# q and k kept as whole fp32 numbers in a hybrid attention and Fourier layer: one fp32 product on quarters of the array in place of three split products

## The reference

```python
h = rmsnorm(x, norm_g)
proj = h @ w_in                       # q, k, v, g_attn, u, g_four
q = rmsnorm(q.reshape(B, S, 12, 64), q_g)
k = rmsnorm(k.reshape(B, S, 12, 64), k_g)
for window, dil in ((128, 1), (512, 4), (2048, 16)):
    # keys gathered by stride dil, band of 64 on each side of the query
    s = einsum('brnqhd,brnkhd->brnhqk', qb, kb) / 8 + bias
    o, lse = softmax(s) @ v, logsumexp(s)
attn = merge of the three by softmax(lse), times silu(g_attn)
four = Re(fft2(u)) @ w_four, times silu(g_four)
y = x + concat[attn, four] @ w_out
```

## Time and profile before

| | us |
|---|---|
| median of three runs | 3880.73 |
| the profiled execution, time | 3869.16 |
| the profiled execution, span from first to last instruction | 3867.4 |
| setup, weights and first half, up to about 1133 | 1133 |
| second half, up to about 2189 | 1056 |
| attention, first score at 2214.3, last product at 3251.8 | 1037 |
| combine | 616 |

### The profile page before, as it was taken

The page is one execution under the profiler, slowest core; times in us unless marked ns, Lnnn a source line. Parts: engine busy times, 40 slices in busy tenths (PEclk is TensorE's granted clock), DMA queues, the critical chain, the costliest instruction groups (busy, mean ns, idle before and its releaser), DMA issues. The chain is left out here.

```text
span 3867.4 us, 99821 instructions
## 1 busy us (share of the span) xinstructions
PE 3720.9 (96%) x38254; PEld 3216.2 (83%) x38254; DVE 2516.7 (65%) x7654; ACT 1696.7 (44%) x4499; POOL 400.2 (10%) x674
## 2 busy tenths in 40 slices
PE   6999999999979999999999799999999997999999
PEld 5888888888867777778888689999999996888887
DVE  5666666666645344433444479888888887777775
ACT  3333333333322111111111189899898987333332
POOL 0000000000000000000000133424334340000000
PEclk9999999999989999999999899999999998999999
DMA  4445555554447875777555578786777764666665
GB/s 147 168 151 159 169 153 153 170 174 145 149 174 228 253 210 167 196 196 201 152 159 159 153 190 212 181 217 170 212 186 197 202 185 149 235 242 242 242 242 179
DMA packets 607705, 722.43 MB, mean 187 GB/s; under 512 B 38299, under 2 KB 474651, under 8 KB 604732
## 3 DMA queue, kind: packets, MB, share of 16 engines
q1 hardware_dynamic: 607356, 717.55, 62.5%
HBM read 383.67 MB, written 337.94 MB: 187 GB/s over the span
## 5 line engine op out<-in xcount | busy, mean ns | idle before, releaser
L592 PE MATMUL p_ps<-p_w_hi,p_h_hi 128*128 128x512 f32 (+1 forms) x3072 | 1145.9, 373 | 22.4 <-DVE p_w_lo L910 20.9
L592 PE MATMUL p_ps<-p_w_hi,p_h_lo 128*128 128x512 f32 (+1 forms) x3072 | 1118.6, 364 | 0.0
L592 PE MATMUL p_ps<-p_w_lo,p_h_hi 128*128 128x512 f32 (+1 forms) x3072 | 1118.4, 364 | 0.0
L1297 ACT ACTIVATE att_p<-att_p,att_o 128x256 f32<-128x256 f32 (+2 forms) x1728 | 682.7, 467 | 107.3 <-DVE att_o L1355 106.1
L592 PEld LDWEIGHTS p_ps<-p_w_hi,p_h_hi 128*128 128x128 f32 x3072 | 582.8, 190 | 124.5 <-issue 31.1
L592 PEld LDWEIGHTS p_ps<-p_w_hi,p_h_lo 128*128 128x128 f32 x3072 | 582.3, 190 | 92.4
L592 PEld LDWEIGHTS p_ps<-p_w_lo,p_h_hi 128*128 128x128 f32 x3072 | 583.4, 190 | 88.1 <-issue 1.9
L1355 DVE CUSTOM_DVE_ANT_0 att_p<-att_ps_s,att_bias 128x256 f32<-128x256 f32 (+2 forms) x1728 | 560.3, 381 | 47.6 <-PE att_ps_s L1235 42.2
L1268 PE MATMUL att_ps_o<-att_v,att_p_low 128*64 128x65 f32 x6528 | 437.2, 225 | 8.3 <-issue 8.2
L1268 PE MATMUL att_ps_o<-att_v,att_p_high 128*64 128x65 f32 x6528 | 437.7, 225 | 4.4 <-issue 4.4
L1268 PEld LDWEIGHTS att_ps_o<-att_v,att_p_low 128*64 128x64 f32 x6528 | 404.4, 139 | 23.5 <-issue 8.7
(11 more groups left out here) (110 smaller groups left out, 5166.0 us busy)
## 6 DMA issues: line engine op xcount, KB each, us to landing
scratch_qk<-staging SPq DMA_DIRECT2D x72, 1024.0 KB, 5.8
out_o<-scratch_o SPq DMA_DIRECT2D x144, 396.0 KB, 5.3
att_qk_a<-scratch_qk SPq DMA_DIRECT2D x192, 256.0 KB, 4.4
scratch_o<-att_o SPq DMA_DIRECT2D x168, 264.0 KB, 3.3
x<-x SPq DMA_DIRECT2D x48, 512.0 KB, 7.0
scratch_h_t<-p_h_hi SPq DMA_DIRECT2D x48, 512.0 KB, 7.4
scratch_h_t<-p_h_lo SPq DMA_DIRECT2D x48, 512.0 KB, 6.4
p_h_hi<-scratch_h_t SPq DMA_DIRECT2D x48, 512.0 KB, 4.2
```

The source lines that it names most:

```text
L592: ins = pe.matmul(ps[c][:, 0:width[c]], a[s][:, k, :], b[:, k, cols], start=(k == 0 and n == 0), stop=(k == KC - 1 and n == 2))
L1297: ins = act.activation(at, at, ACT.Exp, bias=o[n % BUFS][:, (2 * q + i) % STRETCH, PW + e:PW + e + 1], scale=-1.0)
```

## The change

q and k are no longer split. In the first stage ACT alone copies the turned chunk out (`qk_out`), `qk_lo` is gone from DVE, and `store_qk` moves 512 KB. In the attention stage a region has two parts, q and k, and there are two regions of each kind; a pair uses the one of its parity, so that the next pair's can be filled at any time of the present one. A region takes 8 transfers for b and 16 for a: b's go out in rounds 12 to 19 and a's in rounds 20 to 35, one transfer a round. `score` does one plain fp32 product for a head, in two halves of 64 queries: half h of head e goes to columns 64h to 64h+63 and rows 64e to 64e+63 of the array. A step has 8 matmuls in place of 12. The keys' and queries' order in memory is as before. The output stage differs only in how it names `qk_b`.

```diff
-                   "qk": [P, 4 * PAIRS, TOKENS], ...
+                   "qk": [P, 2 * PAIRS, TOKENS], ...
-        core.qk_b = core.sb(core.keep, "qk_b", [P, 4, SEQS[1]], F32R)
+        core.qk_b = core.sb(core.keep, "qk_b", [P, 2, 2, SEQS[1]])
...
-                sp.wait_ge(qk_lo_done, t * 3 + (c - 2))
-                sp.dma_start(dram["qk"][:, 8 * c:8 * c + 8, bass.ds(t * P - 2 * P, 2 * P)],
+                sp.wait_ge(qk_done, t * 3 + (c - 2))
+                sp.dma_start(dram["qk"][:, 4 * c:4 * c + 4, bass.ds(t * P - 2 * P, 2 * P)],
...
-            def qk_lo(t, s, c):
-                dve.wait_ge(qk_hi_done, t * 3 + (c + 1))
...
-A_PIECES, B_PIECES = 32, 16
+A_PIECES, B_PIECES = 16, 8
...
-        qk_a = sb("qk_a", [P, 4, SEQS[0]], F32R)
+        qk_a = sb("qk_a", [P, 2, 2, SEQS[0]])
-        q_packed = [sb(f"q{i}", [P, 2, 2, P], F32R) for i in range(RING)]
+        q_packed = [sb(f"q{i}", [P, 2, P]) for i in range(RING)]
...
-                    if g < 8:
-                        for i in range(2):
-                            load_piece_of("a", it, A_PIECES // 2 + 2 * g + i)
+                    if g < A_PIECES // 2 and opening:
+                        load_piece_of("a", 0, A_PIECES // 2 + g)
...
-                    if 12 <= g < 12 + B_PIECES:
-                        if more:
-                            load_piece_of("b", it + 1, g - 12)
...
-                    if g >= 28 and more:
-                        for i in range(2):
-                            load_piece_of("a", it + 1, 2 * (g - 28) + i)
+                    if more and g >= ROUNDS - A_PIECES - B_PIECES:
+                        i = g - (ROUNDS - A_PIECES - B_PIECES)
+                        load_piece_of("b" if i < B_PIECES else "a", it + 1, i if i < B_PIECES else i - B_PIECES)
...
-                    have = region[parts[place(q)].name]
-                    query = u.queries(have[:, 0:2, :]) if u.dil == LANES else q_packed[q % RING][:, i]
-                    for n, (x, y) in enumerate(((0, 2), (0, 3), (1, 2))):
+                    have = region[parts[place(q)].name][:, pair_of(it, q) % 2]
+                    query = u.queries(have[:, 0, :]) if u.dil == LANES else q_packed[q % RING][:, i]
+                    for h in range(2):
+                        cols = slice(HD * h, HD * (h + 1))
                         for e in range(2):
                             rows = slice(HD * e, HD * (e + 1))
-                            ins = pe.matmul(ps_s[q % 2][e][:, 2 * P * i:2 * P * i + u.w],
-                                            query[rows, x, :], u.keys(have[rows, y, :]),
-                                            start=(n == 0), stop=(n == 2))
+                            ins = pe.matmul(ps_s[q % 2][e][cols, 2 * P * i:2 * P * i + u.w],
+                                            query[rows, cols], u.keys(have[rows, 1, :]), start=True, stop=True)
```

More of the change, by code:

```diff
@@ L115, in build @@
         scratch = {"h_t": [TILES, P, 2 * KC * P], "gate": [TOKENS, D], "ab": [TOKENS, 2 * DF], "four": [TOKENS, DF], "w_out": [D, D],
-                   "qk": [P, 4 * PAIRS, TOKENS], "line": [len(DILS), NH, P * LINE], "bias": [2, P, NH, 2 * P],
+                   "qk": [P, 2 * PAIRS, TOKENS], "line": [len(DILS), NH, P * LINE], "bias": [2, P, NH, 2 * P],
                    "o": [len(DILS), TOKENS, PAIRS, OW],
@@ L707, in qk_hi @@
                 have = ps_qk[(3 * s + c) % 2][:].rearrange("p (b t) -> p b t", t=P)
-                n_q = max(0, PAIRS - 4 * c)
+                n_q = min(4, max(0, PAIRS - 4 * c))
+                to = qk_t[:, 4 * c:4 * c + 4, s * P:(s + 1) * P]
                 if n_q:
-                    ins = act.activation(qk_t[:, 4 * c:min(4 * c + 4, PAIRS), 0, s * P:(s + 1) * P].bitcast(F32R),
-                                         have[:, 0:min(n_q, 4), :], ACT.Copy)
+                    ins = act.activation(to[:, 0:n_q, :], have[:, 0:n_q, :], ACT.Copy)
                 if n_q < 4:
-                    ins = act.activation(qk_t[:, 4 * c + n_q:4 * c + 4, 0, s * P:(s + 1) * P].bitcast(F32R),
-                                         have[:, n_q:4, :], ACT.Copy, scale=gain_qk[:])
-                ins.then_inc(qk_hi_done, 1)
+                    ins = act.activation(to[:, n_q:4, :], have[:, n_q:4, :], ACT.Copy, scale=gain_qk[:])
+                ins.then_inc(qk_done, 1)
             def values(t, s, c):
@@ L785, in _ @@
             if half == 0:
-                qk_hi(TILES - 1, 1, 2)
+                qk_out(TILES - 1, 1, 2)
         @block.vector
@@ L881, in step @@
                 if half == 0:
-                    if not first(t):
-                        qk_lo(t - 1, 1 - s, 2)
                     for c in range(3):
@@ L891, in step @@
                             dve.tensor_copy(ut[:], ps[3][:, DF:2 * DF]).then_inc(ut_copied, 1)
-                        if c == 1:
-                            qk_lo(t, s, 0)
                         if c == (2 if first(t) else 1):
@@ L900, in step @@
                             dve.tensor_copy(ab[s][:], ps[3][:]).then_inc(out_done[3], 1)
-                    qk_lo(t, s, 1)
                 else:
@@ L925, in _ @@
             tiles(dve, step)
-            if half == 0:
-                qk_lo(TILES - 1, 1, 2)
 def region_piece(core, name, region, pair, i):
     base = BASES["ab".index(name)]
-    lanes, part = i // 4, i % 4
+    lanes, part = i // 2, i % 2
     at = slice(lanes * BANK, (lanes + 1) * BANK)
-    return (region[:, part, at].bitcast(F32),
-            core.dram["qk"][:, bass.ds(pair * 2 + (part // 2 * 2 * PAIRS + part % 2), 1),
-                            base + at.start:base + at.stop].rearrange("p a t -> p (a t)"))
+    return (region[:, pair % 2, part, at],
+            core.dram["qk"][:, pair + part * PAIRS, base + at.start:base + at.stop])
 class Unit:
@@ L971, in queries @@
             at = self.r * (rows.shape[-1] // LANES) + self.m * P
-            return rows[:, :, at:at + P]
+            return rows[:, at:at + P]
         shared = LANES // self.dil
-        lanes = rows.rearrange("p x (s c j) -> p c x j s", s=shared, c=self.dil)[:, self.r]
+        lanes = rows.rearrange("p (s c j) -> p c j s", s=shared, c=self.dil)[:, self.r]
         at = self.m * P // shared
-        return lanes[:, :, at:at + P // shared, :]
+        return lanes[:, at:at + P // shared, :]
 class Stretch:
@@ L1146, in body @@
                         load_values(n + 2 - len(parts), it + 1, k)
[L1147 to L1149 removed]
+                    if g < A_PIECES // 2 and opening:
+                        load_piece_of("a", 0, A_PIECES // 2 + g)
                     if g == 0 and not opening:
                         load_bias(2, it)
[L1152 to L1156 removed]
+                    if more and g >= ROUNDS - A_PIECES - B_PIECES:
+                        i = g - (ROUNDS - A_PIECES - B_PIECES)
+                        load_piece_of("b" if i < B_PIECES else "a", it + 1, i if i < B_PIECES else i - B_PIECES)
+                    if not more and 12 <= g < 12 + 2 * KC and g % 2 == 0:
+                        load_w_out((g - 12) // 2)
                     if g in (20, 28) and more:
                         load_bias(0 if g == 20 else 1, it + 1)
[L1159 to L1161 removed]
             load_bias(0, 0)
@@ L1167, in _ @@
                     if n == 0:
-                        for i in range(4):
-                            load_piece_of("a", 0, 4 * k + i)
+                        for i in range(2):
+                            load_piece_of("a", 0, 2 * k + i)
                 load_bias(n + 1, 0)
@@ L1191, in pack @@
                 for i, u in enumerate(two(q)):
-                    ins = pool.tensor_copy(q_packed[q % RING][:, i].rearrange("p x (j s) -> p x j s", s=LANES // u.dil),
-                                           u.queries(region[name][:, 0:2, :]))
+                    ins = pool.tensor_copy(q_packed[q % RING][:, i].rearrange("p (j s) -> p j s", s=LANES // u.dil),
+                                           u.queries(region[name][:, pair_of(it, q) % 2, 0, :]))
                 ins.then_inc(packed, 1)
```

33 lines of the change are left out of this document (10 added, 23 removed).

## The result

The changed kernel takes 3935.17 us (median of 4 runs, 3933.22 to 3941.42), the kernel before beside it 3877.95 (4 runs, 3870.76 to 3884.15): ratio 1.0151, 95% interval 1.0128 to 1.0173. It is 57 us slower, where the prediction had 19. The profiled execution takes 3936.79 us (span 3935.0), 67.6 more than the one of before. The direction was as predicted, and so were the terms that the prediction worked out; a further term of the size of the largest of them was missing from it.

A forecast was written before the change was run, and what follows sets the result against it. PE was taken to bound attention, ACT following at 89%. Terms +50 - 25 - 3.5 - 2.5 = +19 us on the profiled 3869.16 gave 3888, or 3900 on the median; the 8-in-10 range was 3835 to 3955.

The forecast's parts named there:

- Price of a quarter product: Attention scores: a plain fp32 product of 256 columns on a quarter of the array takes 0.429 us.
- Four side by side: Attention scores: a unit's four products run together, each on its quarter, so a round takes 1.716 us at 256 columns.
- rival 2: Attention scores: the four products run only two at a time, +317 us, 4217; chance 0.12.
- Changes of shape: Between scores and turns: two more changes of array shape a round, 0.15 us each, 0.30 us a round.
- Rival 1: Between turns and scores: the new changes of shape cost nothing, so 58 us go, 3842; chance 0.20.
- By stretch: Score blocks: dilation 1 +13, dilation 4 +28, dilation 16 in a +9, in b 0 (end -5); sum +50 us.
- Strided keys: Score products: reading keys in short runs costs 0, with 0 and +60 us kept as ends.
- Rival 3: Scores of dilation 1: the reading of keys binds, +30 to +60 us, 3930 to 3960; chance 0.10.
- Regions: Changes from region b to a: five of six PE waits go, with the lower clock behind them; -25 us.
- Edges: Start of attention -3.5 us (wait for first values), end of the first stage -2.5 us.
- DVE's 192 steps: First stage: the `qk_lo` steps on DVE cost nothing beside a busy PE, so removing them brings nothing.
- PE's own work fills: Attention rounds: PE's transposes, v records, scores and shape changes fill a round of 4.77 us.

The follow-up runs named there:

- wide: The changed kernel with each head's product made once for 128 queries instead of twice for 64, 4 matmuls a step for 8; 3839.01 us, ratio 0.9881.
- quiet: The changed kernel without any load of q, k or v from the second pair on; 3891.33 us, ratio 1.0007.
- noload: The changed kernel without the loads of q and k for the second to the sixth pair; 3923.02 us, ratio 1.0100.
- shift64: The changed kernel with 64 more TensorE instructions (waits already met) once before attention; 3928.78 us, ratio 1.0111.
- shift128: The changed kernel with 128 more TensorE instructions (waits already met) once before attention; 3939.93 us, ratio 1.0135.
- wide_256: The wide kernel with two tiny plain products ahead of each unit's scores, 32 more TensorE instructions a round; 4009.14 us, ratio 1.0344.
- before_pad16: The kernel before with 16 more TensorE instructions in each round, as waits already met; 4129.84 us, ratio 1.0638.

## Why the size was wrong, by the steps of the prediction

- **Price of a quarter product.** Forecast 0.429 us for a unit of 256 columns, 1.716 a round; measured 1.889 with one change of shape in it, and 1.782 without (wide), so 0.445 a unit. Right to 4%.
- **Four side by side.** Right; rival 2 (3.43 us a block, 4217) is dead. It had the support of the page TensorE: Matmul & The Clock Gate of the Trainium skill, Part 3 (Packing small matmuls), that matmuls start strictly in program order. If the two records of a product are neighbours in the program, as the rival took them, this trace disagrees with it for matmuls on different tiles: four records start within 0.02 us, the next four 0.27 us behind them. The order of the compiled program itself is in no trace.
- **Changes of shape.** 0.15 us each and 0.30 a round were charged; comparison with wide gives 0.26. Ahead of the scores the stand-off is in the records: the last one of a turn starts at 2699.80, the first score at 2699.96, 0.15 us where the step is 0.06. Rival 1 (3842) is dead. The page TensorEngine Tiling (Array Packing) of the Trainium skill, Key Properties, says that a change of tiling mode drains TensorE, and this stand-off agrees with it. The kernel wide has no such change between turns and scores, and takes 3839.
- **By stretch.** A full round of dilation 1 took 0.11 us more in its score block and 0.18 in the two turns, 0.29 for a forecast of 0.22; of dilation 4, 0.39 and 0.18, 0.57 for 0.53. By the median of the six pairs at each place, scores and turns together: dilation 1 +19 us for +13, dilation 4 +29 for +28, dilation 16 in a +11 for +9, in b -2 for 0 to -5, 57 in all. The weighing gives 6 back, where the base kernel waits at three places in most pairs and the changed one does not. So the +50.8 that meets the +50 is in part luck.
- **Strided keys.** Taken as 0, and it is 0: the two dilations take 1889 ns alike. Rival 3 is dead; the 0.28 us by which dilation 1 was slower went away with the rounded products, and wide, which has 1.78 for dilation 1, shows it as well.
- **Regions.** -25 for five waits; -24. Right, the lower clock included. That nothing else is late there was not quite so: at the fourth change PE waits 1.6 us for DVE.
- **Edges.** The wait of 3.49 us is gone, the opening score comes after 24.98 us of idle and not 25.6, and the second half restarts 3.2 us sooner: this row of the changed kernel stands for 1149.19 in the earlier trace rows.

```profile
1146.01 0.55 PE L591 MATMUL p_ps<-p_w_hi,p_h_hi 128*128 128x256 f32 x1 [12.28 <-DVE p_w_lo L889]
```

  Together the edges bring 7.6 us where I had 6.
- **DVE's 192 steps.** 93 us of DVE's work went and PE's first stage did not move by 0.1 us. Right.
- **The step that failed** is that "PE's own work fills" the round, so that the sum 50 - 25 - 3.5 - 2.5 could leave out any time in which PE stands for its own instructions: that term was put at nothing without a reason. The page of before showed 246 transfers of instructions, and the waits of before 15.4 us of PE idle for issue, of which only the 3.5 of the earlier trace rows were taken up. The change puts 64 instructions where 48 were, which takes 256 of them from about 5.00 to 4.92 us although the round is longer, and their transfer starts 0.3 us later: the stops cost 48 us more. The sum with this term, 19 + 48 = 67 for 67.6 in the profiled executions, is no second proof, as the 48 are what the other terms leave; the stops themselves are, and the runs quiet and wide, which lose most of them in two different ways.

What stays open: why the transfer of instructions starts later in the changed kernel (2.1 against 1.8 us), which moves fewer bytes in all. In wide, which has the changed kernel's transfers and an eighth fewer matmul instructions, it starts nearly as late (2.0), which points to the order of the transfers rather than to the instructions; no run tests it. That other transfers delay it is shown (quiet, noload); that the place in the round plays a part too is likely (shift64, shift128); which of SP's transfers it stands behind was not taken apart. That length and start together make the stops is shown at both ends, not in between.

## What to carry to other kernels

Before you split a matmul so that its pieces fill the array, ask whether the whole one already does: here 128 stationary columns took no longer than 64, so four products of 64 x 64 are two of 64 x 128 with twice the instructions. Where PE is the bound, count its instructions a microsecond as well as its busy time: idle for "issue" inside a row of like matmuls, just behind the end of a transfer of the instruction queue, is the program not arriving, and here it grew where 256 instructions took less time and where the transfer engines were busier. A sum over medians finds such a term in the trace after; in the trace before it is visible as a small number that may grow.

## What the hardware showed beyond that

- Short matmuls are dear. Eight moving columns in place of none cost 0.22 us for each pair of plain 64 x 128 products (0.89 us a round in wide_256, four pairs), half of what 256 columns cost (0.445), and 0.12 us for four quarter products. Timeline of PE in wide_256, units of 192 columns and the tiny pair ahead of each:

```profile
2780.49 0.28 PE L1207 MATMUL att_ps_s<-ident,att_qk_a 64*128 64x8 f32 x4
2780.63 0.57 PE L1211 MATMUL att_ps_s<-att_qk_a 64*128 64x192 f32 x4
2781.04 0.28 PE L1207 MATMUL att_ps_s<-ident,att_qk_a 64*128 64x8 f32 x4
2781.18 0.57 PE L1211 MATMUL att_ps_s<-att_qk_a 64*128 64x192 f32 x4
```

- A wait that is already met isn't free on TensorE: 0.076 us an instruction between busy blocks (1.2 us for 16, before_pad16), 0.079 us in a row of 64 (5.1 us, shift64) and 0.11 us in a row of 128 (14.2 us, shift128). That two waits make one instruction is in the counts: 256 waits more in shift128 are 128 instructions more in its trace.
